# A warmed-up start, a reordered first group and gating stage, and the norms' logarithm taken from PSUM, in a two-block layer on one core

## The chip, the cores and the metric

The kernel runs on one core of one Trainium2 chip. The metric is device time of the whole program in microseconds (us). Before the change it is 2627.98 us, the median of 3 runs (2627.77 to 2628.41).

## What is computed

512 tokens of width 2048 pass through two blocks, all in float32. Cut to what matters:

```
h = rmsnorm(x, norm_mix_g)                       # first block
u = h @ w_in                                     # 12288 columns: c_g b_g xa za q fl iv og ga gb
ya = b_g * dwconv3(c_g * xa) * silu(za)
o  = hgrn2_chunked(silu(q), (1-lb)*sigmoid(-fl), iv, log_f(fl))      # 8 heads of 128
yb = rmsnorm_per_head(o) * hg_norm_g * silu(og)
m  = sigmoid(ga) * (ya @ w_a_out) + sigmoid(gb) * (yb @ w_b_out)
x  = x + m @ w_o
gate = sigmoid(rmsnorm(x, ple_norm_g) @ w_ple_gate)                  # the gating stage
x  = x + gate * (p @ w_ple_proj)
x  = rmsnorm(x, final_norm_g)
mod = silu(c) @ w_ada + b_ada                                        # second block
h = rms_norm(x, g) * (1 + scale) + shift
proj = h @ w_in2                                 # q k v z of 8 attention and 4 retention heads
y = [dilated_attention * silu(z_a), retention (rms-normed per head) * silu(z_r)]
out = rms_norm(x + gate2 * (y @ w_out2), final_gain)
```

rmsnorm(x) is x times the reciprocal square root of (mean of x squared, plus 1e-6), times a gain.

## The kernel before, in words

**Layout.** Everything is kept transposed: the 2048 features lie in 16 tiles ("rows" k) of 128 partitions by 512 tokens. A norm therefore sums over partitions, which TensorE does with a matrix of ones.

**Dense groups.** Each matrix product is cut into groups of 512 output columns, that is four PSUM banks i = 0 to 3 of 128 columns each. A group walks over its input rows k (16 of them as a rule). To keep float32 accuracy with the fast fp32r format, weights and operand are each split into a high and a low part, and each (k, i) takes three matmuls: j = 0 operand-high times weight-high, j = 1 operand-low times weight-high, j = 2 operand-high times weight-low. A group of 16 rows is thus 192 matmuls. `pe_dense` (L299 to 334) writes them; every one has line L329.

**Units.** Weights come in units n of two rows (128 partitions by 1024 elements, 512 KB). SyncE loads a unit into one of four RAW slots, ScalarE casts it into WH (L354; the very first unit in two halves, L347 and L349), VectorE subtracts to get WL (L375, L369). There are three WH/WL slots, so the cast of unit m waits until TensorE has used unit m-3. `hi_upto`, `lo_upto` and `load_upto` (L201 to 211) say how far each engine is to be with its units at step k of group unit n.

**Operand feeds.** The operand of a group is split in the same way: XH on ScalarE, XL on VectorE. For the first group ("fl", half 0) the raw x is fed before its norm is known (L454, L475); ScalarE also squares x (L459) and VectorE adds the squares up (L483), and the factor R0 is put on the result afterwards. From group ("q", 0) on the normed h is fed (L490, L500, L504). A group that is written with `fed=True` takes its rows k = 0 and 1 singly, since they have only just been fed.

**Order.** There is no scheduler at run time. Each engine's program is a Python generator that writes its instructions in a fixed order, and all waits are on semaphores, so an instruction that waits holds up everything behind it on its engine. Side work is woven in by `Turns.after_step`: after each step k of a dense group one piece of the queue `chores` and one piece of the queue `specials` is written. `start_part` (L513) is the special of the start: seven pieces of operand feed, then on ScalarE and VectorE the small work on the bound lb (`bound_act`, `bound_dve`, L540 to 567), then the first norm, then the feed of h.

**Norms.** `rsqrt_act` and `rsqrt_dve` (L402 to 420) share the reciprocal root: VectorE makes m = mean + eps from PSUM (L412), ScalarE takes Ln of m (L406) and Exp of -0.5 times that (L408), and VectorE makes one Newton step in three operations (L415, L417, L420). The table of Ln and Exp is loaded (L64) after the wait for m. Norms are "r0" (start), "hn" (8 heads), "r_ple" (before the gate), "r_12" and "r_1" (after the gating stage), "rn" (4 retention heads); "r_out" (L1752 to 1779) is written out by hand in two halves at the end.

**The gating stage.** Four groups ("gate", g). Behind each, ScalarE makes four sigmoids (L1630), VectorE multiplies and adds them into x (L1922, L1926). For g = 0 to 2 ScalarE then squares each new row twice (L1650), and GpSimd adds the squares into two sums (L2019); there is one pair of buffers, so each square waits for GpSimd's last addition. Only then does ScalarE's program come to the next group's casts. Behind g = 2 VectorE makes five small weight tiles WG (L1929 to 1935). Behind g = 3 ScalarE squares the last four rows (L1637), TensorE sums everything for "r_12" (L399, L1454, L1457) and "r_1", the norm follows, VectorE makes the gains GG and GF (L1939 to 1943), and the feed of the next group ("qr", 0) begins (L1095, L1080, L1100).

## Time and profile before

| | |
|---|---|
| median of 3 runs | 2627.98 us |
| the profiled execution | 2625.84 us, its span 2624.5 us |
| granted TensorE clock, mean | 0.998 |
| VectorE, ScalarE, GpSimd busy | 48%, 34%, 3% of the span |
| DMA | 309 MB, 118 GB/s on average |
| casts of weight units (ScalarE L354) | 443, 1049 ns each |
| low parts of weight units (VectorE L375) | 443, 1230 ns each |

In the profile, PE is TensorE's matmul, PEld its weight load, DVE VectorE, ACT ScalarE, POOL GpSimd and SP SyncE. A matmul's record is longer than its share of the engine, since matmuls overlap: the distance from one start to the next is what counts. The number in brackets behind a row of the timeline is the engine's idle time before the instruction and what ended it. A float32 matmul (not fp32r) shows as two records.

### The profile page before, as it was taken

The page shows a single profiled execution, that of the slowest core. Times are in us where ns is not written, and L with a number is a line of the kernel's source. Part 1 is how long each engine was busy: PE and PEld are TensorE (multiplying, and loading weights), DVE is VectorE, ACT ScalarE, POOL GpSimd, SP SyncE. Part 2 cuts the span into 40 slices and gives each one's busy share as a digit, 9 for nine tenths or more (in the row PEclk, how much of TensorE's full clock was granted, in tenths as well). Part 3 has the DMA queues.
Part 4 walks back from the last instruction along what each step waited for, and adds up shares of the span by engine and source line. Part 5 has one row for each costly group of instructions (what it writes and reads, how often), then busy time and mean ns, then how long its engine had stood idle before and what let it go on. Part 6 is the DMA issues. An engine that isn't in the chain of part 4 may idle for free.

```text
span 2624.5 us, 29678 instructions
## 1 busy us (share of the span) xinstructions
PE 2593.7 (99%) x12166; PEld 2095.4 (80%) x12166; DVE 1265.5 (48%) x2013; ACT 892.0 (34%) x1236; POOL 73.7 (3%) x64
## 2 busy tenths in 40 slices
PE   8999999999999999999999999999999999999998
PEld 7888888878888888888888888688777777777888
DVE  7556634468334555655443453552243434443425
ACT  5643324333222222222322443332232343433323
POOL 0000000000000000000001111100000000000000
PEclk9999999999999999999999999999999999999999
DMA  5322233222334666666442222234222222222424
GB/s 194 101 76 78 81 97 97 89 73 81 89 96 147 217 216 207 216 213 213 136 161 97 94 99 97 73 125 145 85 72 64 89 72 81 73 73 84 165 97 153
DMA packets 159976, 309.18 MB, mean 118 GB/s; under 512 B 11040, under 2 KB 15392, under 8 KB 158816
## 3 DMA queue, kind: packets, MB, share of 16 engines
q1 hardware_dynamic: 159040, 305.70, 36.1%
q8 instruction: 96, 1.57, 0.2%
q0 software_dynamic: 224, 1.15, 0.1%
q10 hardware_dynamic: 576, 0.43, 0.1%
q14 instruction: 40, 0.33, 0.0%
HBM read 298.84 MB, written 8.39 MB: 117 GB/s over the span
## 4 chain that ended last, share of the span: by engine, by line
PE 94%; DVE 2%; issue 2%; ACT 1%; DMA 0%; POOL 0%; SPq 0%; DVEq 0%; ACTq 0%; POOLq 0%
PE bank L329 87%; PE bank L1276 1%; PE bank L1167 1%; PE bank L1250 1%; PE bank L702 1%; PE bank L754 1%; PE bank L1265 1%; PE bank L1156 1%; PE bank L399 0%; DVE WL L375 0%; ACT WH L354 0%; DVE SC L483 0%; DMA X<-in_xT 0%; DVE Y L1980 0%; PE bank L692 0%
## 5 line engine op out<-in xcount | busy, mean ns | idle before, releaser
L329 PE MATMUL bank<-XH,WH 128*128 128x512 f32 (+1 forms) x2880 | 1145.6, 398 | 12.2 <-DVE XL L475 5.5
L329 PE MATMUL bank<-XH,WL 128*128 128x512 f32 (+1 forms) x2880 | 1111.7, 386 | 5.5 <-DVE WL L375 5.5
L329 PE MATMUL bank<-XL,WH 128*128 128x512 f32 (+1 forms) x2880 | 1109.9, 385 | 0.0
L375 DVE TENSOR_TENSOR WL<-RAW,WH 128x1024 fp32r<-128x1024 f32 x443 | 544.0, 1230 | 958.1 <-ACT WH L354 957.2
L354 ACT CAST WH<-RAW 128x1024 fp32r<-128x1024 f32 x443 | 463.9, 1049 | 1162.2 <-PE bank L329 1162.0
L329 PEld LDWEIGHTS bank<-XH,WH 128*128 128x128 f32 x2880 | 542.4, 188 | 135.1 <-issue 20.7
L329 PEld LDWEIGHTS bank<-XL,WH 128*128 128x128 f32 x2880 | 542.7, 188 | 119.3 <-issue 15.0
L329 PEld LDWEIGHTS bank<-XH,WL 128*128 128x128 f32 x2880 | 542.1, 188 | 116.9 <-DVE WL L375 7.2
L329 PE MATMUL bank<-WH,XH 128*128 128x512 f32 x384 | 155.6, 405 | 0.0
L329 PE MATMUL bank<-WL,XH 128*128 128x512 f32 x384 | 149.8, 390 | 0.0
L329 PE MATMUL bank<-WH,XL 128*128 128x512 f32 x384 | 149.5, 389 | 0.0
L1016 DVE CUSTOM_DVE_ANT_0 AST<-AST,CB 128x512 f32<-128x512 f32 x192 | 125.3, 687 | 10.8 <-DMA AST<-in_w_ada 10.8
L329 PE MATMUL bank<-YH,WH 128*128 128x512 f32 x256 | 101.0, 394 | 0.0
L329 PE MATMUL bank<-YH,WL 128*128 128x512 f32 x256 | 100.4, 392 | 0.0
L329 PE MATMUL bank<-YL,WH 128*128 128x512 f32 x256 | 99.5, 389 | 0.0
L329 PEld LDWEIGHTS bank<-WH,XL 128*128 128x128 f32 x384 | 72.2, 188 | 17.5 <-issue 3.1
L329 PEld LDWEIGHTS bank<-WH,XH 128*128 128x128 f32 x384 | 72.1, 188 | 17.4 <-issue 3.1
L329 PEld LDWEIGHTS bank<-WL,XH 128*128 128x128 f32 x384 | 72.1, 188 | 15.3
L1354 DVE CUSTOM_DVE_ANT_0 PP<-PP,CM 128x512 f32<-128x512 f32 x32 | 22.2, 692 | 79.9 <-ACT PP L1288 79.9
L1305 ACT COPY PT<-bank 128x512 f32<-128x512 f32 x32 | 18.7, 585 | 116.1 <-PE bank L1265 116.1
L329 PEld LDWEIGHTS bank<-YH,WL 128*128 128x128 f32 x256 | 48.1, 188 | 11.3
L329 PEld LDWEIGHTS bank<-YL,WH 128*128 128x128 f32 x256 | 48.1, 188 | 10.7
(252 smaller groups left out, 1634.5 us busy)
## 6 DMA issues: line engine op xcount, KB each, us to landing
RAW<-in_w_in SPq DMA_DIRECT2D x303, 512.0 KB, 3.6
AST<-in_w_ada SPq DMA_DIRECT2D x192, 256.0 KB, 4.1
RAW<-in_w_out SPq DMA_DIRECT2D x40, 512.0 KB, 3.5
RAW<-in_w_o SPq DMA_DIRECT2D x32, 512.0 KB, 3.5
RAW<-in_w_gate SPq DMA_DIRECT2D x32, 512.0 KB, 3.5
RAW<-in_w_a SPq DMA_DIRECT2D x16, 512.0 KB, 4.2
RAW<-in_w_b SPq DMA_DIRECT2D x16, 512.0 KB, 4.2
XT<-in_xT SPq DMA_DIRECT2D x4, 1024.0 KB, 7.4
```

The lines of the kernel that those rows point to most:

```text
L329: ins = nc.tensor.matmul(bank[b][:, cols], l, r[:, cols], start=first, stop=final)
L354: nc.scalar.copy(WH[:, m % NSPL], RAW[:, m % NRAW]).then_inc(hi.sem, hi.step(m))
L375: nc.vector.tensor_tensor(WL[:, m % NSPL], RAW[:, m % NRAW], WH[:, m % NSPL].bitcast(F32), ALU.subtract).then_inc(lo.sem, lo.step(m))
L702: ins = nc.tensor.matmul(b[y:y + 64, 32 * n:32 * n + 32].rearrange("p (n x) -> p n x", x=h), t, late(t, lev), start=True, stop=True, tile_ ...
L754: ins = nc.tensor.matmul(b[:, 128 * c:512], VN[:, c, 128 * i:128 * i + 128], AT[:, 640 * c:512 * c + 512], start=c == 0, stop=c == 3)
L1016: nc.vector.tensor_tensor_reduce(AST[:, n % 3], AST[:, n % 3], CB[:, q % 2], 1.0, 0.0, ALU.mult, ALU.add, PART[:, n:n + 1]).then_inc(dve.s ...
L1156: nc.tensor.matmul(b[:, :], YY[:, 9 + 2 * r, 128 * c:128 * c + 128], YY[:, 8 + 2 * r], start=True, stop=True).then_inc(side.sem, side.step ...
L1167: ins = nc.tensor.matmul(b[:, :], V2[:, c, 256 * r + 128 * u:256 * r + 128 * u + 128], PT[:, c], start=c == 0, stop=c == 3)
L1250: nc.tensor.matmul(b[:, :], YY[:, h, 128 * i:128 * i + 128], K[:, j], start=True, stop=True).then_inc(side.sem, side.step(("as", h, i)))
L1265: ins = nc.tensor.transpose(b[:, 128 * c:128 * c + 128], PP[:, i % 2, 128 * c:128 * c + 128], IDN[:, :])
L1276: ins = nc.tensor.matmul(b[:, :], Vt[:, c, 128 * j:128 * j + 128], PT[:, c], start=c == 0, stop=c == 3)
L1354: nc.vector.tensor_tensor_reduce(P, P, CM[:, 2, 384 - 128 * i:896 - 128 * i], 1.0, 0.0, ALU.mult, ALU.add, st[:, 2:3]).then_inc(dve.sem, d ...
```

## The change

It does these things:

- It gives the first three units an order of their own (`hi_upto`, `lo_upto`): one unit is cast and subtracted per step k while n < 2.
- Row k = 0 of every `fed` group is written with j outermost: four matmuls of j = 0, then four of j = 1, then four of j = 2. The wait for the operand's low part moves from j = 0 to j = 1.
- TensorE begins with 11 matmuls of 128x128 ones by 128 columns of ones, into a bank that nothing else uses then.
- The start's feed is spread over ten pieces instead of seven, with one row less of lead (`ahead` 1 instead of 2), the squares of x have four buffers instead of two and are written one row later, and the first norm is written before the work on the bound instead of after it.
- Norms: ScalarE's Ln reads the sum in PSUM, with scale and with eps as a bias from a small tile EPSV; VectorE's m is written after a wait for that Ln. The table load is written before the wait.
- The gating stage: the squares of g = 0 to 2 become a chore woven into the next group; the WG tiles become a chore of the second group; GG and GF are made before the first gate group.

```diff
 def hi_upto(n, k):
+    if n < 2:
+        return k + 1
     return min(n + AHEAD if n or k else 0, len(UNITS) - 1) + 1
 def lo_upto(n, k):
-    return min(hi_upto(n, k), n + AHEAD + k % 2 if n else 3)
+    return hi_upto(n, k) if n < 2 else min(hi_upto(n, k), n + AHEAD + k % 2)
...
-            if fed and k < 2:
-                work = [(k, i) for i in range(4)]
+            if fed and k == 0:
+                work = [(0, i, (j,)) for j in range(3) for i in range(4)]
+            elif fed and k == 1:
+                work = [(1, i, (0, 1, 2)) for i in range(4)]
...
-                for j, (l, r) in enumerate(pairs):
+                for j in parts:
+                    l, r = pairs[j]
                     if j == 0:
...
-                        T.wait_ge(xlo, (yield xlo, (ready, kk)))
...
+                    if j == 1:
+                        T.wait_ge(xlo, (yield xlo, (ready, kk)))
...
-    def rsqrt_act(key, m, y):
-        A.wait_ge(dve, (yield dve, (key, "m")))
+    def rsqrt_act(key, scale, y, eps=0):
         A.use(LNEXP)
-        nc.scalar.activation(y, m, ACT.Ln).then_inc(act.sem, act.step((key, "ln")))
+        A.wait_ge(side, (yield side, (key, "sum")))
+        A.wait_ge(dve, (yield dve, "eps"))
+        nc.scalar.activation(y, bank[banks[key]][:, :], ACT.Ln, bias=EPSV[:, eps:eps + 1], scale=scale
+                             ).then_inc(act.sem, act.step((key, "ln")))
...
     def rsqrt_dve(key, scale, m, y, t, eps=EPS):
-        V.wait_ge(side, (yield side, (key, "sum")))
+        V.wait_ge(act, (yield act, (key, "ln")))
...
+    SQ_AT = (0, 1, 3, 4)
...
-            for j in range(k - 1 if k else 16, 16 if k == 15 else k):
-                if j > 2:
-                    A.wait_ge(dve, (yield dve, ("acc0", j - 2)))
-                nc.scalar.activation(SC[:, j % 2 if j else 2], X0[:, j], ACT.Square
+            for j in range(max(k - 2, 0) if k < 11 else k - 1, 16 if k == 15 else k if k > 9 else k - 1):
+                if j > 4:
+                    A.wait_ge(dve, (yield dve, ("acc0", j - 4)))
+                nc.scalar.activation(SC[:, SQ_AT[j % 4] if j else 2], X0[:, j], ACT.Square
...
     def start_part(eng, bound, norm):
-        for n in range(7):
+        for n in range(10):
             if eng in raw_feed:
-                yield from raw_feed[eng].upto(min(16, 2 * n + 4))
-            yield
-        if bound:
-            yield from bound
-        yield
+                yield from raw_feed[eng].upto(2 * n + 2 if n < 4 else 4 + (4 * n + 1) // 3)
             yield
         if eng == "pe":
             yield
         yield from norm
         yield
+        if bound:
+            yield from bound
...
     def pe():
+        T.wait_ge(dve, (yield dve, "ones"))
+        for n in range(11):
+            nc.tensor.matmul(bank[7][:, 0:128], ONES[:, :], ONES[:, :], start=True, stop=True)
...
-        yield from act_dense(("fl", 0), raw_feed["act"])
+        yield from act_dense(("fl", 0), raw_feed["act"], 1)
...
-            for i in range(4):
-                j = 4 * g + i
-                A.wait_ge(dve, (yield dve, ("x2", j)))
-                if g == 3:
+            if g < 3:
+                turns.chores.append(squares_act(g))
+                continue
+            yield from turns.finish(turns.chores)
...
+    def squares_act(g):
+        for j in range(4 * g, 4 * g + 4):
+            A.wait_ge(dve, (yield dve, ("x2", j)))
+            for u in range(2):
+                scale = vcol("fin_g", j) if u else 1.0
...
+                    if j > 1:
+                        A.wait_ge(pool, (yield pool, ("acc2u", u, j - 1)))
...
+                nc.scalar.activation(dst, X1[:, j], ACT.Square, scale=scale
+                                     ).then_inc(act.sem, act.step(("sq2u", u, j)))
+            yield
+            yield
...
     def out_norm_act(h):
-        A.wait_ge(dve, (yield dve, ("r_out", h, "m")))
-        nc.scalar.activation(N2[:, 1, HALF[h]], N2[:, 0, HALF[h]], ACT.Ln
+        A.wait_ge(side, (yield side, ("r_out", h, "sum")))
+        nc.scalar.activation(N2[:, 1, HALF[h]], bank[banks["r_out", h]][:, HALF[h]], ACT.Ln, bias=EPSV[:, 0:1],
...
     def out_norm_dve(h):
-        V.wait_ge(side, (yield side, ("r_out", h, "sum")))
+        V.wait_ge(act, (yield act, ("r_out", h, "ln")))
...
+        nc.vector.memset(EPSV[:, 0:1], EPS).then_inc(dve.sem, dve.step())
+        nc.vector.memset(EPSV[:, 1:2], EPS * EPS).then_inc(dve.sem, dve.step("eps"))
...
+        V.wait_ge(dve, (yield dve, "mod"))
+        nc.vector.tensor_scalar(GG, MOD[:, 16:32], 1.0, None, ALU.add).then_inc(dve.sem, dve.step("gg0"))
...
+        nc.vector.tensor_tensor(GF, GG, vall("fin_g"), ALU.mult).then_inc(dve.sem, dve.step("gf"))
         for g in range(4):
...
-            if g == 2:
-                nc.vector.tensor_scalar(WG[:, 4], ONES[:, :], EPS, None, ALU.mult
...
+            if g == 0:
+                turns.chores.append(last_weights_dve())
+        yield from turns.finish(turns.chores)
```

`last_weights_dve` waits four steps and then makes the same nine small operations, two or three a step. Squares of the last four rows stay where they were, directly behind the sigmoids of g = 3.

## Rows read from the trace of the kernel before

**Rows 1.** Page, part 1: busy time, share of the span, instructions of each engine.

```profile
PE 2593.7 (99%) x12166; PEld 2095.4 (80%) x12166; DVE 1265.5 (48%) x2013; ACT 892.0 (34%) x1236; POOL 73.7 (3%) x64
```

**Rows 2.** Waits of PE: total us, times, longest us.

```profile
PE bank L329 <- DVE WL L375: 5.5, 4, 2.3
PE bank L329 <- DVE XL L1100: 4.7, 2, 4.3
...
PE bank L329 <- ACT WH L354: 0.5, 2, 0.3
```

**Rows 3.** Timeline, the start and two small float32 matmuls: start us, us, instruction.

```profile
0.84 0.17 DVE L1818 MEMSET ONES<- 128x128 f32 x1 [0.84 <-PEq L2158]
...
4.42 0.60 ACT L347 CAST WH<-RAW 128x512 fp32r<-128x512 f32 x1
...
5.53 0.77 PE L329 MATMUL bank<-XH,WH 128*128 128x512 f32 x1 [5.53 <-DVE XL L475]
...
9.50 0.40 PE L329 MATMUL bank<-XH,WH 128*128 128x512 f32 x1
...
174.33 0.38 PE L719 MATMUL bank<-XX 128*128 128x128 f32 x2
174.55 0.39 PE L720 MATMUL bank<-XX 128*128 128x128 f32 x2
```

**Rows 4.** Windows: span, busy us (x records) of each engine, PEclk, DMA share, GB/s.

```profile
5.50:9.50 4.00, 3.97 (x10) 3.14 (x10) 1.95 (x4) 2.61 (x5) 0.00 (x0) 1.00 1.04 392
...
1699.00:1702.40 3.40, 3.40 (x8) 2.75 (x9) 3.40 (x5) 1.45 (x2) 0.00 (x0) 0.51 0.00 0
...
1505.80:1549.80 44.00, 44.00 (x195) 36.42 (x195) 26.29 (x34) 19.16 (x27) 0.00 (x0) 1.00 0.31 108
```

**Rows 5.** Timeline, first group: the stop near its end, and the first row of h.

```profile
35.17 0.39 PE L329 MATMUL bank<-XL,WH 128*128 128x512 f32 x1
...
37.87 0.51 PE L329 MATMUL bank<-XH,WL 128*128 128x512 f32 x1 [2.31 <-DVE WL L375]
...
45.86 1.29 DVE L500 TENSOR_TENSOR X<-X,R 128x512 f32<-128x512 f32 x2
```

**Rows 6.** Timeline, the third gate group's start, and GpSimd in the stage's last.

```profile
1603.63 2.92 ACT L354 CAST WH<-RAW 128x1024 fp32r<-128x1024 f32 x3
...
1606.60 0.50 PE L329 MATMUL bank<-XH,WL 128*128 128x512 f32 x1 [1.15 <-DVE WL L375]
...
1640.31 10.65 POOL L2019 TENSOR_TENSOR AC<-AC,SQ 128x512 f32<-128x512 f32 x8 [34.85 <-ACT SQ L1650]
```

**Rows 7.** Timeline, the norm "r_12" behind the gating stage.

```profile
1685.78 2.41 ACT L1637 ACTIVATE SQ<-X 128x512 f32<-128x512 f32 x4
...
1690.43 0.69 DVE L412 TENSOR_SCALAR NN<-bank 128x512 f32<-128x512 f32 x1 [2.91 <-PE bank L1457]
1691.15 1.28 ACT L64 ACT_TABLE_LOAD   x1 [2.96 <-DVE NN L412]
1692.44 0.63 ACT L406 ACTIVATE NN<-NN 128x512 f32<-128x512 f32 x1
...
1693.77 0.69 DVE L415 TENSOR_TENSOR NN<-NN 128x512 f32<-128x512 f32 x1 [2.64 <-ACT NN L408]
...
1695.83 0.17 DVE L1939 TENSOR_SCALAR SM<-MOD 128x16 f32<-128x16 f32 x1
...
1696.45 1.41 DVE L1095 SCALAR_TENSOR_TENSOR GT<-X,SM,NN 128x512 f32<-128x512 f32 x2
1697.24 1.38 ACT L1080 ACTIVATE XH<-GT,MOD 128x512 fp32r<-128x512 f32 x2 [2.57 <-DVE GT L1095]
...
1699.00 0.70 PE L329 MATMUL bank<-XH,WH 128*128 128x512 f32 x1 [4.31 <-DVE XL L1100]
```

**Rows 8.** Timeline, the last norm, second half.

```profile
2613.51 0.42 DVE L1769 TENSOR_SCALAR N<-bank 128x256 f32<-128x256 f32 x1 [1.68 <-PE bank L1504]
2613.97 0.42 ACT L1758 ACTIVATE N<-N 128x256 f32<-128x256 f32 x1 [1.69 <-DVE N L1769]
```

More of the change, by code:

```diff
@@ L304, in pe_dense @@
             s = n % NSPL
-            if fed and k < 2:
-                work = [(k, i) for i in range(4)]
-            else:
-                work = [(k - k % 2 + j, i + k % 2 * 2) for i in range(2) for j in range(2)]
-            for q, i in work:
+            if fed and k == 0:
+                work = [(0, i, (j,)) for j in range(3) for i in range(4)]
+            elif fed and k == 1:
+                work = [(1, i, (0, 1, 2)) for i in range(4)]
+            else:
+                work = [(k - k % 2 + j, i + k % 2 * 2, (0, 1, 2)) for i in range(2) for j in range(2)]
+            for q, i, parts in work:
                 kk = kmap[q] if kmap else q
@@ L330, in pe_dense @@
                     done = [(name, i)] * (j == 2 and q == nk - 1)
-                    done += [("unit", n)] * (j == 2 and k % 2 == 1 and (q, i) == work[-1])
+                    done += [("unit", n)] * (j == 2 and k % 2 == 1 and (q, i) == work[-1][:2])
                     if done:
@@ L820, in hgrn_act @@
         yield
-        yield from rsqrt_act(("hn", hh), XX[:, 0], XX[:, 1])
+        yield from rsqrt_act(("hn", hh), 1.0 / 128, XX[:, 1])
         yield
@@ L1204, in retention_act @@
         yield
-        yield from rsqrt_act(("rn", r), TN[:, 2], TN[:, 3])
+        yield from rsqrt_act(("rn", r), 1.0 / 256, TN[:, 3])
         left.discard(r)
@@ L1631, in act_program @@
                                      ).then_inc(ev_a.sem, ev_a.step((("gate", g), i)))
[L1632 to L1652 removed]
+            if g < 3:
+                turns.chores.append(squares_act(g))
+                continue
+            yield from turns.finish(turns.chores)
+            A.wait_ge(dense, (yield dense, (("proj", 3), 3)))
+            for i in range(4):
+                A.wait_ge(dve, (yield dve, ("x2", 12 + i)))
+                nc.scalar.activation(SQ2[:, 2 + i], X1[:, 12 + i], ACT.Square
+                                     ).then_inc(act.sem, act.step(("sq2", 12 + i)))
+        yield from rsqrt_act("r_12", 1.0 / D, R12, 1)
         turns.specials.append(first_norm_act())
@@ L1752, in act_program @@
                 yield from to_end(out_norm_act(1))
+    def squares_act(g):
[3 more added lines that the diff above has]
+                scale = vcol("fin_g", j) if u else 1.0
+                if j == 0:
+                    A.wait_ge(side, (yield side, ("r_ple", "sum")))
+                    dst = AC[:, u]
+                else:
+                    A.wait_ge(dense, (yield dense, (("proj", 3), 3)))
+                    if j > 1:
+                        A.wait_ge(pool, (yield pool, ("acc2u", u, j - 1)))
+                    dst = SQ2[:, u]
+                nc.scalar.activation(dst, X1[:, j], ACT.Square, scale=scale
+                                     ).then_inc(act.sem, act.step(("sq2u", u, j)))
+            yield
+            yield
     def out_norm_act(h):
@@ L1808, in first_norm_act @@
         yield from idle(4)
-        yield from rsqrt_act("r_1", NN[:, 0], R1)
+        yield from rsqrt_act("r_1", 1.0 / D, R1)
     def first_norm_dve():
@@ L1814, in first_norm_dve, with last_weights_dve @@
         yield from rsqrt_dve("r_1", 1.0 / D, NN[:, 0], R1, NN[:, 2])
+    def last_weights_dve():
+        yield from idle(4)
+        nc.vector.tensor_scalar(WG[:, 4], ONES[:, :], EPS, None, ALU.mult
+                                ).then_inc(dve.sem, dve.step())
+        for i in range(4):
+            nc.vector.tensor_scalar(WG[:, i], ONES[:, :], vcol("fin_g", 12 + i), vcol("fin_g", 12 + i),
+                                    ALU.mult, ALU.mult).then_inc(dve.sem, dve.step(("wg", i)))
+            V.wait_ge(dve, (yield dve, ("wg", i)))
+            nc.vector.tensor_scalar(WG[:, i], WG[:, i], EPS, None, ALU.add
+                                    ).then_inc(dve.sem, dve.step(*(["wg"] if i == 3 else [])))
+            yield
     def dve_program():
```

45 lines of the change are left out of this document (10 added, 35 removed).

## The prediction, made before the changed kernel was run

> **What bounds the kernel now.** I read the page first: TensorE is busy 99% of the span [rows 1]. So the kernel can gain only where TensorE stands still or runs slowly, and where its end is followed by a tail. The waits of PE come next. They are few: low parts of weights (L375) stop it four times, ScalarE's casts (L354) twice, the low part of an operand behind the gating stage (L1100) twice [rows 2]; the first matmul starts only at 5.53 [rows 3]. The timeline then puts each in its place. Of the four stops by L375, one of 2.31 us is in the first group [rows 5] and three are in the gating stage, with both stops by L354 [rows 6]; of L1100's 4.7 us, 4.31 is the norm "r_12" [rows 7].
>
> Two things are not in a list of waits. In full flow a matmul takes 0.226 us (44.00 us by 195) [rows 4]. From 5.53 to 9.50 [rows 3] there are nine intervals, 0.44 each; the window's PEclk says 1.00 there, but the ten records in 4 us say half speed [rows 4]. Behind the stop of 4.31 us, eight matmuls fill 3.40 us, and there PEclk says 0.51 [rows 4], that is 1.2 of 2.4 GHz. The stop of 2.31 us was followed by nothing of the kind: the row behind it is 0.51 long, as a first one after a stop is, against 0.39 [rows 5]. So TensorE starts slowly after 5.5 and 4.3 us of standing still, and not after 2.3. A stop costs its idle time and some 0.27 more: from 35.17 to 37.87 is 2.70, less 0.226 is 2.47 against 2.31 idle, and 0.12 for the longer first record [rows 5].
>
> **The start.** The 11 added matmuls need only ONES, ready at 1.01 [rows 3]. A float32 matmul of 128 columns takes 0.22 at full speed (174.33 to 174.55, two records each) [rows 3], so twice that, 0.44, at half: 11 of them end at 1.1 + 4.8 = 5.9 if all are slow. If full speed comes as it did at 9.50, some 4.0 us behind the first matmul, it comes at 5.1, nine are slow and two fast, and they end near 5.4 (estimate). The first real matmul no longer waits for the operand's low part; it needs the high part of the weights, ready at 5.02 [rows 3]. I take 5.4: 0.1 us gained (ends: 0.4 later, 0.5 earlier), and the nine slow intervals gone: 3.97 - 9 x 0.226 = 1.94. At full speed the group asks more of its feeds. It wants row 1 at 5.4 + 2.7 = 8.1 and rows 2 and 3 at 10.8; with units 1 and 2 cast one by one instead of together, unit 1's low part is ready near 9.4, and a gap there would be under 0.5.
>
> The stop at 37.87 goes if unit 5's low part comes in time. Before, VectorE wrote all 16 rows of feed and then unit 5; now only 12 rows stand ahead of it, four fewer at about 1.3 us (a low part and an addition). Taken off the 37.87, that is 32.7, and TensorE asks at 5.4 + 10 x 2.72 + 0.45 = 33.1; the shorter queues of ScalarE (four square buffers) help too. Gain 2.47 + 0.12 = 2.6; low end 1, should unit 5 or 6 still come 1 to 1.5 us late.
>
> The norm's place gives a new wait. VectorE and ScalarE now stand at the norm while unit 7's low part is behind it. From the sum's being visible that takes 0.73 (Ln), 0.66, 3 x 0.72 and 1.2 for the unit, 4.8 in all; TensorE needs it two steps and a part later, 5.4 + 0.45, and 0.2 of hand-over go off: 0.9 to spare. The feed of h began at 45.86 [rows 5] and will begin at about the same time, since the bound's ten small operations, some 0.2 us each as L1939's 0.17 [rows 7], now follow the norm, while group ("q", 0) starts 4.6 us earlier. Its first low parts of weights have 0.7 to 0.8 us left by my count of the queue. I take no stop; 0.5 to 1 of one is the low end. Sum of the start: 0.1 + 1.9 + 2.6 = **4.6** (2.5 to 5.1).
>
> **The gating stage.** At 1603.63 ScalarE casts three units in a row. Units fall due 5.4 us apart (24 matmuls), so the first could have come some 9 us sooner; the squares had held it, each waiting for GpSimd's addition of 1.33 us (10.65 by 8) [rows 6]. With the squares woven in, the cast comes right behind the sigmoids, and the next squares, two every second step (5.4 us), need 2.7 us of GpSimd: no wait left. VectorE's nine WG operations leave the boundary behind g = 2; in the second group they stand before units that are due two units later. All five stops go: 5.5 - 2.3 = 3.2 by L375, 0.5 by L354 [rows 2], 5 x 0.27: **5.0** (4 to 5.1). GG and GF, 0.6 us on VectorE, move ahead of the gate groups, where low parts of the operand are several rows ahead.
>
> **The norm "r_12".** Now: the sum is there at 1690.43, m, then a table load at 1691.15, Ln at 1692.44, Newton at 1693.77, GG at 1695.83, first gained row at 1696.45, its high part at 1697.24, matmul at 1699.00 [rows 7]. After: the squares end at 1688.19 [rows 7], the load (1.28) fits before 1690.43; Ln and Exp take 1.33 as between 1692.44 and 1693.77, plus 0.07 for the bias operand, which no row prices (I take it between nothing and 0.15); Newton starts at 1691.8, and three steps of 0.72 later, without GG and GF, the gained row starts at 1694.0. Its high part starts 0.79 later as now and takes 0.72; with 0.2 of hand-over TensorE starts at 1695.7, as it no longer waits for the low part, which is ready when four matmuls are done. Gain **3.3** (2.3 if it does have to wait for the low part).
>
> ScalarE's page of the Trainium skill, "ScalarE: Activation LUTs", section What ACT_TABLE_LOAD costs, speaks against part of this: a switch costs 1283 ns and some 1380 ns of drain. By it the table would be ready at 1690.85 and the gain 0.4 smaller. The trace agrees on 1.28 but shows no drain: Ln starts 0.01 behind the load [rows 7].
>
> TensorE's sums of "r_1" end at 1694.7, so the stop shrinks from 4.31 to about 1.0, well below the 2.31 that left it fast: the slow stretch goes too, 3.40 - 8 x 0.226 = **1.6**. The second stop by L1100, 0.4 and 0.27, stands behind "r_1", whose chain on VectorE gets shorter by the 1.3 us (Ln and Exp) it waits between m and Newton: **0.6**.
>
> **The tail.** In the last norm Ln starts when m does now, 2613.51 instead of 2613.97 [rows 8]; less 0.1 for the bias: **0.4**, all on the path. The other norms lie beside dense groups in which TensorE never waits: nothing. The j-outermost order asks for the fourth bank of a group 1.4 us earlier; in group "wb", the only one that takes banks of the group just before, its fourth bank was that group's second, complete 12 matmuls (2.7 us) before the start, and a read takes some 0.6: nothing.
>
> **Sum.** 4.6 + 5.0 + 3.3 + 1.6 + 0.6 + 0.4 = 15.5. The profiled execution, 2625.84 with a span of 2624.5, would become 2610.3 and 2609.0. It lies 2.1 under the median of the runs, and I take the difference off that: 2627.98 - 15.5 = **2612.5**.
>
> **Rivals.** (a) The warm-up does not warm: small matmuls leave the clock low, they end at 5.9 and the first nine real ones are slow as before. Gain 15.5 - 1.9 - 0.5 = 13.1: 2614.9. For it: no row shows what 128-column matmuls do to the clock. Against: they fill the engine from 1.1 on. Chance 0.12. "TensorE: Matmul & The Clock Gate", Part 1, in the Trainium skill says that the number of slow matmuls varies from run to run with the phase of the gate. By that this term scatters; a single profile of before cannot show it. (b) The first group becomes VectorE's: with TensorE 4.6 us ahead, unit 5, 7 or 8 stops it as before, 2 to 3 us. For it: VectorE is the engine that stopped it at 37.87, and my slack is under 1 us at three places. Against: it has idle time in which to catch up. 2612.5 + 2.5 = 2615.0. Chance 0.18. (c) A part of what is said does not come: one gating stop stays or "r_12" gains only half. 2614 to 2618. Chance 0.13. (d) Slower: the squares woven in stand ahead of the casts, in all three later gate groups, and wait there for GpSimd. Each of 12 pieces has at most 2.7 us of additions to wait for, and a cast has some 9 us before TensorE needs it. To cost more than the 15.5 gained, 12 pieces would have to bring 1.3 us each past that slack, so each wait would be above 10 us. It decides only if VectorE's x2 rows came a whole unit late, which they do at no boundary now. Some 2633 with a wait of that size. Chance 0.02. (e) The edits do nothing for the time because something else stops TensorE at the same places: within 0.2%. Chance 0.03.
>
> **The numbers.** The likeliest case, as worked out, has 0.52. A run of this kernel can be told from no change at about 0.2%, 5.3 us; all of (a) to (c) are faster than that. So faster 0.95, same 0.03, slower 0.02. The range: above, it takes in (a), (b) and most of (c), 2618.0; below, the upper ends of the terms (0.5 at the start, a bit in the small stops) and some scatter of the median, 2610.0.
>
> **What would show it.** Right: first real matmul near 5.4 at 0.23 intervals; no stop above 0.3 us before 60 us; in the waits of PE no L354 and no L375 in the gating stage; casts directly behind the sigmoids; a table load before the sum and a stop under 1.3 us before ("qr", 0), with PEclk near 1 behind it; Ln straight behind the last sum. Wrong: intervals of 0.43 behind the warm-up (a), a wait for L375 between 8 and 60 us (b), squares ahead of a late cast (d), or new waits of TensorE for banks at the first row of a `fed` group.

## The result, and the profile after

The changed kernel takes **2613.57 us**, the median of 4 runs (2612.94 to 2613.85), beside 2628.19 for the kernel before in the same session (4 runs, 2627.77 to 2630.15). The ratio is 0.9943, with a 95% interval of 0.9925 to 0.996. That is 14.6 us less; forecast were 15.5 less and 2612.5. The two profiled executions differ by less: 2625.84 and 2613.68, that is 12.2, and their spans by 12.7 (2624.54 and 2611.86). The text below works with this 12.7 of span and comes back to the difference between 14.6 and 12.2.

The page of the changed kernel, part 1 (busy time, share of the span, instructions; before: [rows 1]):

```profile
PE 2595.7 (99%) x12188; PEld 2097.1 (80%) x12188; DVE 1260.2 (48%) x2015; ACT 889.0 (34%) x1236; POOL 79.0 (3%) x64
```

TensorE is now busy for 2.0 us longer than before, with a span that is 12.6 shorter. Eleven small matmuls of at most 0.43 us are 4.7 of that; but nine slow intervals at the start and eight behind "r_12" have gone, 3.5 together. Something else has become longer.

The waits of PE in the changed kernel (total us, times, longest; before: [rows 2]):

```profile
PE bank L1273 <- ACT PP L1305: 2.0, 2, 1.0
PE bank L336 <- DVE Y L2006: 1.5, 2, 1.2
PE bank L1415 <- DVE EPSV L1850: 1.1, 1, 1.1
PE bank L336 <- issue: 0.9, 1, 0.9
```

L336 is the dense matmul (L329 before). No wait for weights' low parts (now L382) or casts (L361) is left, and none for the operand's low part. The first two stops, in the attention stage and the last groups, are not touched by the change; the third is the start of the program; 0.9 is what remains of the 4.31 at "r_12".

The timeline of the changed kernel at its start (start us, us, instruction; before: [rows 3]), and VectorE's low part of unit 5 (before: in [rows 5] as the releaser of the stop):

```profile
1.06 5.00 PE L1415 MATMUL bank<-ONES 128*128 128x128 f32 x22 [1.06 <-DVE EPSV L1850]
...
4.64 0.60 ACT L354 CAST WH<-RAW 128x512 fp32r<-128x512 f32 x1
...
5.77 1.22 PE L336 MATMUL bank<-XH,WH 128*128 128x512 f32 x4
6.83 1.09 PE L336 MATMUL bank<-XL,WH 128*128 128x512 f32 x4
7.76 1.10 PE L336 MATMUL bank<-XH,WL 128*128 128x512 f32 x4
...
29.60 1.22 DVE L382 TENSOR_TENSOR WL<-RAW,WH 128x1024 fp32r<-128x1024 f32 x1
```

All 11 warm-up matmuls went at half speed: 4.71 us from 1.06 to 5.77, 0.43 each. The real ones are fast nearly from the first: four in 1.06, then four in 0.93. The weights' high part had been ready at 5.24, so it was the warm-up that the first real matmul waited for.

The timeline of the changed kernel at "r_12" (before: [rows 7]), and a window behind it (span, then busy us and records of each engine, PEclk, DMA share, GB/s; before: [rows 4]):

```profile
1682.94 1.28 ACT L64 ACT_TABLE_LOAD   x1
...
1685.18 0.69 ACT L414 ACTIVATE NN<-bank,EPSV 128x512 f32<-128x512 f32 x1 [0.95 <-PE bank L1468]
...
1686.56 0.69 DVE L424 TENSOR_TENSOR NN<-NN 128x512 f32<-128x512 f32 x1
...
1688.74 1.41 DVE L1103 SCALAR_TENSOR_TENSOR GT<-X,SM,NN 128x512 f32<-128x512 f32 x2
1689.53 1.39 ACT L1088 ACTIVATE XH<-GT,MOD 128x512 fp32r<-128x512 f32 x2 [2.06 <-DVE GT L1103]
1690.28 0.75 DVE L1108 SCALAR_TENSOR_TENSOR XL<-GT,MOD,XH 128x512 fp32r<-128x512 f32 x1
1690.35 1.17 PE L336 MATMUL bank<-XH,WH 128*128 128x512 f32 x4 [0.92 <-issue]
1691.35 1.08 PE L336 MATMUL bank<-XL,WH 128*128 128x512 f32 x4
```

```profile
1690.30:1693.70 3.40, 3.35 (x15) 2.79 (x16) 3.40 (x6) 1.99 (x3) 0.00 (x0) 1.00 0.00 0
```

In the first, the table load stands before the sum, Ln directly behind it, and the operand's low part is begun only 0.07 before the first matmul, which no longer waits for it. Fifteen matmuls in 3.40 us at PEclk 1.00 stand where there were eight at 0.51.

Where the 12.7 come from is seen by laying the starts of the same groups in the two traces beside each other:

| stretch | lead gained, us | predicted |
|---|---|---|
| first matmul (5.77) | -0.24 | +0.1 |
| the rest of the first two groups (to 95.1) | 3.57 | 4.5 |
| to 824 | 0.53 | 0 |
| 824 to 1505.7: eight groups "wa"/"wb" and the projection | **-3.72** | 0 |
| gating stage, "r_12", "r_1" (to 1777.5) | 10.74 | 10.5 |
| attention stage and last groups | 1.36 | 0 |
| tail | 0.44 | 0.4 |

The norm, gating and tail terms fit. A loss of 3.7 us stands where the change edits nothing. One such group, first the kernel before, then the changed one (windows from the group's first matmul to the next group's):

```profile
827.95:849.94 21.99, 21.99 (x97) 18.05 (x96) 12.32 (x24) 5.31 (x6) 0.00 (x0) 1.00 0.71 228
```

```profile
824.09:846.50 22.41, 22.41 (x97) 18.02 (x96) 12.37 (x24) 5.32 (x6) 0.00 (x0) 1.00 0.71 226
```

The same 96 matmuls, the same clock, no idle time in either, and 0.42 us more: 0.2334 instead of 0.2290 for each. What the change did here is hidden in its memory layout. EPSV takes 32 bytes, and the region behind it, W0, moves from byte 127424 to 127456 of each partition. These groups' operands YH and YL lie in W0, as do those of the first group.

### The profile page after: what moved, and what is told of

It reads as the page before. It is cut to its first block, busy times and chain, and to the rows that moved or that the text cites. A ratio compares the mean times of both kernels' runs of the same rounds, so it can differ in the third digit from the quotient of the medians.

```text
span 2611.9 us, 29663 instructions
## 1 busy us (share of the span) xinstructions
PE 2595.7 (99%) x12188; PEld 2097.1 (80%) x12188; DVE 1260.2 (48%) x2015; ACT 889.0 (34%) x1236; POOL 79.0 (3%) x64
## 4 chain that ended last, share of the span: by engine, by line
PE 99%; DVE 1%; ACT 0%; issue 0%
PE bank L336 91%; PE bank L1175 1%; PE bank L1284 1%; PE bank L1258 1%; PE bank L710 1%; PE bank L762 1%; PE bank L406 1%; PE bank L1273 1%; PE bank L1164 1%; PE bank L1415 0%; DVE Y L2006 0%; PE bank L700 0%; PE bank L718 0%; DVE X L1803 0%; PE bank L732 0%; PE bank L1515 0%
## 5 line engine op out<-in xcount | busy, mean ns | idle before, releaser
L336 PE MATMUL bank<-XH,WH 128*128 128x512 f32 (+1 forms) x2880 | 1135.3, 396 | 2.4 <-DVE Y L2006 1.5
L336 PE MATMUL bank<-XH,WL 128*128 128x512 f32 (+1 forms) x2880 | 1102.1, 385 | 0.0
L336 PE MATMUL bank<-XL,WH 128*128 128x512 f32 (+1 forms) x2880 | 1102.0, 385 | 0.0
L382 DVE TENSOR_TENSOR WL<-RAW,WH 128x1024 fp32r<-128x1024 f32 x443 | 543.2, 1227 | 959.3 <-ACT WH L361 958.3
L361 ACT CAST WH<-RAW 128x1024 fp32r<-128x1024 f32 x443 | 463.6, 1047 | 1191.3 <-PE bank L336 1187.3
L336 PEld LDWEIGHTS bank<-XH,WH 128*128 128x128 f32 x2880 | 540.8, 188 | 124.8 <-issue 16.9
L336 PEld LDWEIGHTS bank<-XL,WH 128*128 128x128 f32 x2880 | 541.0, 188 | 118.7 <-issue 15.1
L336 PEld LDWEIGHTS bank<-XH,WL 128*128 128x128 f32 x2880 | 540.7, 188 | 108.8
L336 PE MATMUL bank<-WH,XH 128*128 128x512 f32 x384 | 155.3, 404 | 0.0
L336 PE MATMUL bank<-WL,XH 128*128 128x512 f32 x384 | 149.6, 390 | 0.0
L336 PE MATMUL bank<-WH,XL 128*128 128x512 f32 x384 | 149.4, 389 | 0.0
L336 PE MATMUL bank<-YH,WL 128*128 128x512 f32 x256 | 100.1, 399 | 0.0
L336 PE MATMUL bank<-YL,WH 128*128 128x512 f32 x256 | 99.0, 394 | 0.0
L336 PE MATMUL bank<-YH,WH 128*128 128x512 f32 x256 | 98.5, 393 | 0.0
L336 PEld LDWEIGHTS bank<-WH,XL 128*128 128x128 f32 x384 | 72.1, 188 | 17.6 <-issue 3.1
L336 PEld LDWEIGHTS bank<-WH,XH 128*128 128x128 f32 x384 | 72.1, 188 | 17.3 <-issue 3.1
L336 PEld LDWEIGHTS bank<-WL,XH 128*128 128x128 f32 x384 | 72.1, 188 | 15.1
L336 PEld LDWEIGHTS bank<-YL,WH 128*128 128x128 f32 x256 | 48.1, 188 | 12.4
L336 PEld LDWEIGHTS bank<-YH,WH 128*128 128x128 f32 x256 | 48.1, 188 | 11.4
```

The source lines that it names most:

```text
L336: ins = nc.tensor.matmul(bank[b][:, cols], l, r[:, cols], start=first, stop=final)
L361: nc.scalar.copy(WH[:, m % NSPL], RAW[:, m % NRAW]).then_inc(hi.sem, hi.step(m))
L382: nc.vector.tensor_tensor(WL[:, m % NSPL], RAW[:, m % NRAW], WH[:, m % NSPL].bitcast(F32), ALU.subtract).then_inc(lo.sem, lo.step(m))
```

## The experiments

Each expectation sets a theory against a rival. The first four runs ask about the memory layout.

### The layout

**e1_aligned**, the changed kernel with W0 moved on by another 32 bytes:

```diff
-    W0 = C0 + 3712 + 4 * NVEC
+    W0 = C0 + 3744 + 4 * NVEC
```

> The changed kernel with one number altered: the region W0 begins 64 bytes behind where it began before the change, instead of 32. Theory A (address): the 32-byte shift that made room for EPSV costs every matmul whose moving operand lies behind W0 some 4.4 ns; these are the first group (192), the eight wa and wb groups (768) and the four proj groups (96), 1056 matmuls, 4.6 us. Then a wa or wb group takes 21.99 us again instead of 22.41, the lead over the kernel before no longer falls from 3.86 to 0.54 us between 828 and 1309, and the whole is 4 to 5 us faster than the changed kernel, near 2609. Rival B (order): the groups are slower through the new order of the other engines' work, or through the chip of that run; then a wa group still takes 22.41 and the time stays near 2613.5.

Measured: 2615.23 us (2614.85 to 2616.07), ratio 0.9953 [0.9938, 0.9968]. The group "wa" takes as long as in the changed kernel:

```profile
824.48:846.87 22.39, 22.39 (x98) 18.02 (x96) 12.37 (x24) 5.33 (x6) 0.00 (x0) 1.00 0.72 226
```

Some 2609 was forecast: that the operand only needs a rounder start address is refuted. From 1777 to 2206, where the changed kernel gained 0.94, this one lost 0.64: the layout does act, but not by that rule.

**e2_before_shift32**, the kernel before with W0 moved by 32 bytes and nothing else:

```diff
-    W0 = C0 + 3680 + 4 * NVEC
+    W0 = C0 + 3712 + 4 * NVEC
```

> The kernel before with W0 alone moved by 32 bytes. Theory A (address): wa and wb groups take 22.41 us instead of 21.99, the first group loses 0.8 us, proj 0.4; the whole 4 to 5 us slower than before, near 2632.5, a ratio of 1.0017. Rival B (order): nothing changes, 2628 within 0.5.

Measured: 2630.2 us (10 runs, 2628.42 to 2632.28) beside 2627.82 (13 runs, 2626.31 to 2630.77); ratio 1.0007 [0.9997, 1.0017]. That is 2.4 more, where 4 to 5 were forecast, and the ratio alone can't tell it from nothing; the trace can. Against the kernel before it loses 3.72 from 829 to 1511; it gains 0.53 between 100 and 829, and 1.4 from 1795 on (0.94 of them by 2224). All of these are what the changed kernel shows, within 0.02. So the loss belongs to the 32 bytes, not to the edits. The forecast had left out the two gains.

**m1_addresses** measures it by itself. It leaves out the whole computation: 16 fp32r matmuls in a row of one 128x128 weight by 128x512 from one start address, then two small ones, then the next address.

```diff
+        for off in offs:
...
+            for i in range(16):
+                ins = T.matmul(bank[i % 4][:, :], W[:, :], big[key][:, off // 4:off // 4 + 512], start=True, stop=True)
+            for i in range(2):
+                ins = T.matmul(bank[4][:, 0:64 + 64 * i], W[:, :], big[key][:, 0:64 + 64 * i], start=True, stop=True)
```

> The cost by itself: a kernel that only runs fp32r matmuls of 128x512, sixteen in a row per start address of the moving operand, with nothing else at work; it leaves out the whole computation. Addresses: 57472 (where XH lies in the kernels) plus 0, 64, ... 2048 bytes and some others, and 127424 (W0 before the change) plus 0, 32 (the change), 64 (the run with W0 64 bytes on) and others. The runs so far showed 0.2269 us a matmul with the operand in XH, 0.2290 with W0 as before, 0.2334 with W0 32 or 64 bytes on, so alignment to 64 bytes is not it. Theory A2 (place in memory alone): the same three values, or the same order of them, appear here, by the start address modulo some power of two. Rival C (contention): the address matters only by which bank of the memory other engines are writing at the time; then all addresses give the same value here, 0.22 to 0.227.

Its timeline, for starts 128, 192, 0, 64 and 128 behind a multiple of 256 bytes:

```profile
25.81 3.85 PE L52 MATMUL bank<-Near,Wt 128*128 128x512 f32 x16
29.50 0.33 PE L54 MATMUL bank<-Near,Wt 128*128 128x64 f32 x2
29.67 3.89 PE L52 MATMUL bank<-Near,Wt 128*128 128x512 f32 x16
33.40 0.33 PE L54 MATMUL bank<-Near,Wt 128*128 128x64 f32 x2
33.57 3.94 PE L52 MATMUL bank<-Near,Wt 128*128 128x512 f32 x16
37.35 0.33 PE L54 MATMUL bank<-Near,Wt 128*128 128x64 f32 x2
37.52 3.95 PE L52 MATMUL bank<-Near,Wt 128*128 128x512 f32 x16
41.30 0.33 PE L54 MATMUL bank<-Near,Wt 128*128 128x64 f32 x2
41.47 3.85 PE L52 MATMUL bank<-Near,Wt 128*128 128x512 f32 x16
45.16 0.33 PE L54 MATMUL bank<-Near,Wt 128*128 128x64 f32 x2
```

From a row of 16 to the pair behind it, by 16: 0.2306 at 128, 0.2331 at 192, 0.2363 at 0, 0.2363 at 64, and 0.2306 at 128 again. The pattern repeats every 256 bytes; starts at 32, 160 and 224 take 0.2362 to 0.2374, in this buffer or in a second one at 127424. The first matmul of a row, behind the small pair, is followed only after 0.28 to 0.29, and that is in these averages. From the third to the fifteenth the step is 0.2267 at 128 in this buffer (0.2276 to 0.2284 in the other), 0.2291 at 192, and 0.2325 to 0.2345 at all other starts. These are the steps of the kernels: 0.2267, 0.2290 and 0.2334 (below and above). Nothing else runs here, so work of other engines is out as the cause, and a matmul's time depends on where its moving operand starts: W0 stood at 192 before (second best), at 224 after, at 0 in e1.

**e10_w0_128** puts W0 at 128, the best place:

```diff
-    W0 = C0 + 3712 + 4 * NVEC
+    W0 = C0 + 3872 + 4 * NVEC
```

> The changed kernel with the region W0 moved from byte 127456 to 127616, so that it starts at 128 behind a multiple of 256 (192 in the kernel before, 224 in the changed one). Theory A, the start address of the moving operand modulo 256 sets the distance of two matmuls: the operands YH and YL of the eight groups wa and wb then go at the 0.227 us of XH, 96 matmuls take 21.8 instead of 22.4, and 1056 matmuls gain up to 1056 x 0.0065 = 6.9 us against the changed kernel's 2613.6; the attention stage, whose operands move along, may give back up to 1.6. So 2607 to 2610. Rival B, the matmuls of these groups are slow for another reason (what else runs beside them, the bank they write): the groups stay at 22.4 and the time at 2613 or above.

Measured: **2608.08 us** (2607.78 to 2608.6), ratio 0.9925 [0.9908, 0.9941]. The group that took 21.99 before and 22.41 after:

```profile
823.10:844.86 21.76, 21.76 (x97) 18.02 (x96) 12.28 (x24) 5.31 (x6) 0.00 (x0) 1.00 0.73 231
```

That is 0.2267 for each matmul. Between 823 and 1498 this kernel gains 2.43 on the kernel before, where the changed kernel lost 3.72. Part is given back: it gets neither the 0.53 before 824 nor the 0.94 of the attention stage (there -0.23). One base address moves many operands, and they don't agree on the best one. Theory A holds; this version beats both kernels, 5.5 us under the changed one by the medians (two sessions, whose medians of the kernel before were 0.2 apart) and 5.4 by the spans. Of these, 0.5 is a first matmul at 5.31 instead of 5.77, which the address does not explain.

### The start

**e3_no_warm**, without the warm-up:

```diff
-        T.wait_ge(dve, (yield dve, "ones"))
-        for n in range(11):
-            nc.tensor.matmul(bank[7][:, 0:128], ONES[:, :], ONES[:, :], start=True, stop=True)
```

> The changed kernel without the 11 warm-up matmuls. My theory: the first real matmul starts some 0.4 to 0.6 us earlier (5.2 instead of 5.77) and the first nine or so run at 0.43 us intervals, 1.9 us lost: the span is 1.3 to 1.6 us longer. Rival: the warm-up is worth nothing, because the feeds of the first rows set the pace in the first 12 us anyway; then TensorE reaches row 2 at the same time (within 0.3) with or without it, and the span is the same.

Measured: 2614.43 us (2614.08 to 2614.61), ratio 0.995 [0.9935, 0.9964].

```profile
5.06 2.07 PE L336 MATMUL bank<-XH,WH 128*128 128x512 f32 x4 [5.06 <-ACT WH L354]
6.93 1.91 PE L336 MATMUL bank<-XL,WH 128*128 128x512 f32 x4
8.63 1.15 PE L336 MATMUL bank<-XH,WL 128*128 128x512 f32 x4
```

Eight slow intervals, but a start at 5.06. At 96 us it is 0.92 behind the changed kernel, as it is in the medians (0.86): the warm-up is worth 0.9, less than expected, since it wins some 1.7 of slow intervals and gives 0.7 back by a later first matmul.

**e12_w0_warm9**, e10 with nine instead of eleven:

```diff
-        for n in range(11):
+        for n in range(9):
```

> The kernel of e10_w0_128 with 9 warm-up matmuls instead of 11. In the changed kernel all 11 ran at half speed and ended at 5.8, 0.7 us behind the high part of the first weights. Theory A, the clock rises a fixed time after TensorE began: with 9 the first real matmul starts at 5.1, the first two or three real ones take 0.43, and the whole is up to 0.3 us faster than e10. Rival B: the rise needs what the last two warm-ups add; then the first real matmuls are slow for longer, and the time is the same or up to 0.5 us longer than that of e10.

Measured: 2608.57 us (2608.23 to 2609.41), ratio 0.9926 [0.9912, 0.9941], no better than e10. The warm-ups end early and TensorE waits 0.59 for the cast of the first weights; it starts at 5.35, and e10, whose clock rose within its warm-ups, at 5.31. Two short stops in the third row (0.17 at 11.48 by the operand's low part, and one at 12.52) then cost 0.8. The first real matmul can't start before the first weights' cast ends, between 5.0 and 5.5 in these traces, whatever TensorE does.

Theory A of this run, a rise of the clock a fixed time after TensorE began, is refuted by the traces together, and the two missing warm-ups did not hold it back either (rival B). In all kernels with a warm-up it begins at 1.05 or 1.06. By the distances of starts full speed came at 4.1 here, at 4.8 in e10, at the end of the warm-ups in the changed kernel, and only at 7.1 in e4 below, where the first four real matmuls take this long (1.22 in the changed kernel):

```profile
5.77 1.80 PE L336 MATMUL bank<-XH,WH 128*128 128x512 f32 x4
```

At 95 us e4 is 0.55 behind the changed kernel, with no edit there. So what a warm-up of this length is worth differs between executions, by up to half a microsecond in these traces.

**e7_old_first_order**, the changed kernel with the whole old order of the first group (units 0 to 2, seven pieces of feed, the lead of two rows, the norm behind the bound):

```diff
 def hi_upto(n, k):
-    if n < 2:
-        return k + 1
...
-    return hi_upto(n, k) if n < 2 else min(hi_upto(n, k), n + AHEAD + k % 2)
+    return min(hi_upto(n, k), n + AHEAD + k % 2 if n else 3)
...
-        for n in range(10):
+        for n in range(7):
...
-                yield from raw_feed[eng].upto(2 * n + 2 if n < 4 else 4 + (4 * n + 1) // 3)
+                yield from raw_feed[eng].upto(min(16, 2 * n + 4))
```

> The changed kernel with the first group's order of before (units, feed pieces, bound ahead of the norm, lead of 2; warm-up, four square buffers and the j order stay). My theory: the stop behind unit 5's low part comes back, 2 to 4 us, longer than before's 2.3 if anything, because TensorE now runs the group 2 us earlier. Rival: the warm-up and the four square buffers alone were enough; the stop stays under 0.5 us.

Measured: 2615.67 us in one run; 1.9 behind the changed kernel at 95 us, though its first matmul was 0.4 earlier (5.37).

```profile
12.55 0.50 PE L334 MATMUL bank<-XH,WH 128*128 128x512 f32 x1 [1.33 <-ACT WH L359]
12.89 0.39 PE L334 MATMUL bank<-XL,WH 128*128 128x512 f32 x1
13.81 0.50 PE L334 MATMUL bank<-XH,WL 128*128 128x512 f32 x1 [0.53 <-DVE WL L380]
```

The stop that I expected behind unit 5 came at unit 1 instead. With TensorE fast from the start, the old order gives it the weights of rows 2 and 3 too late; in the kernel before, where TensorE was itself slow for 4 us, nothing stopped it there. The delay then hides what unit 5 would have cost: its low part is begun at 34.31 and ready at 35.52, and TensorE asks for it at 36.31. The changed kernel asks at 34.37, so at its pace the stop would be some 1.2 us (estimate).

**e11_two_square_buffers**, the old buffers and rows for the squares of x:

```diff
-            for j in range(max(k - 2, 0) if k < 11 else k - 1, 16 if k == 15 else k if k > 9 else k - 1):
-                if j > 4:
-                    A.wait_ge(dve, (yield dve, ("acc0", j - 4)))
...
+            for j in range(k - 1 if k else 16, 16 if k == 15 else k):
+                if j > 2:
+                    A.wait_ge(dve, (yield dve, ("acc0", j - 2)))
...
```

> The changed kernel with the old two buffers for the squares of x, each square written in its old row. Theory A, the stop of 2.31 us behind weight unit 5 was ended by the squares holding up ScalarE's and VectorE's queues, not by the order of units 0 to 2: a stop of 1 to 3 us by a low part of weights or by a cast comes back between 25 and 45 us, and the lead over the kernel before at 95 us falls from 3.3 to 0.5 to 2.3. Rival B, the spread of the operand feed over ten pieces is what removed it: no stop above 0.3 us there, the lead at 95 us stays at 3.0 to 3.3.

Measured: 2613.74 us in one run; at 95 us 0.57 behind the changed kernel.

```profile
30.79 1.22 DVE L382 TENSOR_TENSOR WL<-RAW,WH 128x1024 fp32r<-128x1024 f32 x1
```

Unit 5's low part is 1.2 us later than with four buffers and still in time; there is no stop. In both, VectorE has made the low parts of 12 rows of x before it, in the kernel before and in e7 those of all 16. So theory A is refuted, and the order of the feed is what is left. That stays argued: e7 took this order back, but its TensorE came too late to need unit 5 early. Of the 0.57, 0.2 are slower first matmuls and 0.4 a later sum of the first norm (40.00).

**e8_j_inner**, row 0 of the `fed` groups in the old order of j:

```diff
-            if fed and k == 0:
-                work = [(0, i, (j,)) for j in range(3) for i in range(4)]
-            elif fed and k == 1:
-                work = [(1, i, (0, 1, 2)) for i in range(4)]
+            if fed and k < 2:
+                work = [(k, i, (0, 1, 2)) for i in range(4)]
```

> The changed kernel with j innermost again in row 0 of the fed groups; the wait for the low part stays at j = 1. My theory: the stop in front of qr is as long (0.9), but behind its first matmul TensorE waits some 0.7 us for the first low part; at the start it costs nothing, as the low parts are there when the warm-up ends. In all 0.5 to 1.0 us slower. Rival: the low part is ready by then and nothing changes.

Measured: 2614.33 us in one run. In the trace 0.9 are lost within the first 60 us, half of them within the first four matmuls, where the third waits for the weights' low part (I had forecast nothing there), and 0.5 at "qr":

```profile
1690.95 0.47 PE L334 MATMUL bank<-XH,WH 128*128 128x512 f32 x1 [0.91 <-issue]
1691.69 0.50 PE L334 MATMUL bank<-XL,WH 128*128 128x512 f32 x1 [0.27 <-DVE XL L1106]
```

TensorE stops for the low part right behind its first matmul, as forecast; the j-outermost order costs nothing anywhere.

### The gating stage and the norm

**e4_squares_back**, the squares directly behind the sigmoids again:

```diff
-                turns.chores.append(squares_act(g))
+                yield from to_end(squares_act(g))
```

> The changed kernel with the squares of the first three gate groups written directly behind the sigmoids again (WG stays a chore). My theory: the squares are what holds the casts, so the five stops come back but the third boundary's longest, to which the WG work added, is like the second's: stops of 0.2, 0.3, 1.15, 0.3 and 1.2 us with 0.27 each, 4.4 us in all. Rival: without the WG work VectorE catches up and the stops stay under 2 us in all.

Measured: 2618.3 us in one run. Its waits of PE:

```profile
PE bank L336 <- DVE WL L382: 2.5, 3, 1.2
...
PE bank L336 <- ACT WH L361: 0.5, 2, 0.3
```

All five stops are back, three for low parts, two for casts; only the one in the last gate group is shorter than before (1.16 for 1.80). From 1505 to 1782 the lead grows by 6.21 instead of 10.73: the squares' place is worth 4.5. Of the 10.7, "r_12" and "r_1" have 5.6 (below). The last 0.6 is the shorter stop in the last gate group (1.16 for 1.80), where the WG tiles had stood in the way; no run moved them back alone.

**e5_ln_from_m**, Ln from VectorE's m, the table load behind the wait, as before:

```diff
     def rsqrt_act(key, scale, y, eps=0):
...
+        A.wait_ge(dve, (yield dve, (key, "m")))
         A.use(LNEXP)
...
+        nc.scalar.activation(y, m, ACT.Ln).then_inc(act.sem, act.step((key, "ln")))
```

> The changed kernel with the norms as before: Ln from m, the table load behind the wait (GG and GF stay ahead of the gate groups; the last norm keeps its new form). My theory: the stop in front of group qr grows from 0.9 to about 2.9 us (0.7 for m, 1.3 for the table load, less the longer bias operand), which is just about where TensorE may or may not slow down; if it does not, the whole is 2 us slower, if it does, 3.6. The stop behind r_1 may come back, 0.3. Rival: the gain at r_12 came from GG and GF and the relaxed wait for the low part, and the norms' form gives under 1 us.

**e6_load_first**, the same with the table load ahead of the wait:

```diff
     def rsqrt_act(key, scale, y, eps=0):
...
         A.use(LNEXP)
...
+        A.wait_ge(dve, (yield dve, (key, "m")))
+        nc.scalar.activation(y, m, ACT.Ln).then_inc(act.sem, act.step((key, "ln")))
```

> The changed kernel with the logarithm taken from VectorE's m again, as before, but the table load still written ahead of the wait for m. In the run that undid both (e5_ln_from_m) 3.9 us were lost at the norm r_12, of them some 1.6 by eight slow matmuls behind a stop of 2.86 us. Theory A, the table load of 1.28 us is most of it and m 0.7 the rest: here 0.6 to 0.8 us are lost at r_12, the stop is 1.6 us and nothing slow is behind it; in all 2614.5 to 2615. Rival B: m costs more because the hand-overs between the engines count too, 1.2 us or more are lost; or the stop of 1.6 us brings slow matmuls as the one of 1.8 us did in a run before, then 2.2 or more.

Measured, one run each: 2617.34 and 2614.08 us. First e5's timeline and window, then e6's:

```profile
1686.17 1.28 ACT L64 ACT_TABLE_LOAD   x1 [2.98 <-DVE NN L422]
1687.47 0.63 ACT L416 ACTIVATE NN<-NN 128x512 f32<-128x512 f32 x1
...
1692.58 1.95 PE L336 MATMUL bank<-XH,WH 128*128 128x512 f32 x4 [2.86 <-issue]
```

```profile
1692.55:1696.05 3.50, 3.47 (x9) 2.74 (x10) 3.50 (x6) 2.04 (x3) 0.00 (x0) 0.52 0.00 0
```

```profile
1690.92 1.17 PE L336 MATMUL bank<-XH,WH 128*128 128x512 f32 x4 [1.58 <-issue]
```

The stop is 0.92 in the changed kernel, 1.58 with m in the way, 2.86 with the load behind it as well: m costs 0.66 and the load 1.28, each its own duration and no more. Behind 2.86 us eight matmuls go at half speed, another 1.6; that makes 3.5 of the 3.9 that e5 loses here. Behind 1.58 all are fast. The last 0.3, lost in e6 too, is the second stop, behind "r_1" (in e6 at 1713.89). So the norms' new form is 1.94 of the 3.39 by which the stop at "r_12" shrank, and the rival that it gives under 1 us is out. The other 1.45 belong to GG and GF and to the relaxed wait for the low part; no run took back GG and GF, and e8 took back only the order of j.

## Why the prediction was right, and where it was not

**The start, 4.6 forecast, 3.3 measured.** Full speed behind the warm-up and no stop to 60 us came as said; rivals (a) and (b) are out, as are (c) to (e): no forecast stop stayed, and none came. Unit 5's low part was ready at 30.82, not at 32.7, behind the 12 rows that I had counted, and TensorE asked for it at 34.37, not at 33.1. "I take 5.4" for the first matmul was wrong, 5.77: I let the clock rise within the warm-ups, and in this execution it rose at their end. In e10's it rose earlier (11 in 4.25 us), in e4's later (7.1): this term was taken from one trace and scatters. The Trainium skill, "TensorE: Matmul & The Clock Gate", Part 1, says that the number of slow matmuls varies from run to run; the traces agree: 9 slow ones in the kernel before, 10 in e2, all 11 small ones here. The later first matmul is 0.3 of the missing 1.3; another 0.8 is the layout, 192 x 0.0044: between 14 and 34 us the first group's steps are 0.2333 instead of 0.2289.

**The gating stage and "r_12", 10.5 forecast, 10.7 measured**, by the steps given: squares 4.5 (e4), the WG tiles 0.6 (together 5.1; 5.0 forecast); the stop from 4.31 to 0.92 (3.4; 3.3 forecast), the slow stretch 1.6, and the second stop, of "r_1", 0.6. Ln from PSUM with a bias operand takes 0.06 more than from m (0.69 against 0.63); m costs 0.66 (e6), the load 1.28 (e5 less e6). The Trainium skill, "ScalarE: Activation LUTs", What ACT_TABLE_LOAD costs, adds 1380 ns of drain to a table switch; no trace here shows it, and in e5 Ln starts 0.02 behind the load. The tail gave 0.44 for 0.4.

**What no step had.** I costed EPSV at nothing. It was the dearest line of the change: 32 bytes in front of W0 cost 0.8 in the first group and 3.7 in the groups behind 824, and gave back 0.5 before 824 and 1.4 from 1777 on, net 2.7 us; the loss and both gains stand in e2's trace, without any of the other edits. 15.5 less 2.7 is 12.8, against the 12.7 of the two spans.

**That the number still fitted** is partly luck: by the profiled pair the saving was 3.3 us less than forecast, by the medians 0.9 less. The medians differ by 14.6, which is 2.4 more than the profiled pair's 12.2. The profiled execution of the kernel before, 2625.84, is below every timed run of it (2626.31 to 2630.77 in all), while the changed kernel's runs lie within 1 us. I had taken the saving off the median unchanged, as though the stops cost the same in every execution. They may not. In e2's trace the last gating stop by a weights' low part, 1.80 us in the kernel before, reads (timeline, then the window behind it):

```profile
1657.98 0.50 PE L329 MATMUL bank<-XH,WL 128*128 128x512 f32 x1 [1.81 <-DVE WL L375]
...
1659.36 0.63 PE L329 MATMUL bank<-XL,WH 128*128 128x512 f32 x1
1659.78 0.63 PE L329 MATMUL bank<-XH,WL 128*128 128x512 f32 x1
```

```profile
1659.36:1662.85 3.49, 3.49 (x10) 2.77 (x9) 0.83 (x1) 0.00 (x0) 0.00 (x0) 0.55 0.89 298
```

Five matmuls behind the stop the clock fell: nine intervals fill 3.64 us (1659.01 to 1662.65) instead of 2.0, so 1.6 more. In the profiled execution of the kernel before it did not. So "slowly after 5.5 and 4.3 us of standing still, and not after 2.3" was drawn from too few stops. Such stretches in some executions would explain both the scatter of the kernel before and the 2.4 us, since the changed kernel has no gating stop left to bring one. The timed runs speak for it. The record gives the mean granted clock of each execution, and a stretch of 3.4 us at half speed takes 0.0006 off the mean over 2627 us. Of the 21 executions of the kernel before that were timed beside the experiments, the five at 0.998 took 2626.31 to 2626.81 us, the fifteen at 0.997 took 2627.59 to 2629.39, and the one at 0.996 took 2630.77; the profiled one, 2625.84, had 0.998. So the spread goes with the clock. Where the slow stretches lay in those executions is not shown, since no run profiled the same kernel many times.

## What to carry to other kernels

In a kernel that TensorE fills, compare the starts of the same groups in both traces before believing a sum: a new 8-byte tile in front of a large region can move a thousand matmuls to a worse start address. Put moving operands where short runs show them to be fastest, and re-measure, since operands in one region may want different places. What the clock adds to a stop differs between executions, so a single profile doesn't price it: look at the granted clock of the timed runs too.

## What the runs showed of the hardware that I had not expected

- A 128x512 fp32r matmul takes 0.227 us from a start 128 bytes behind a multiple of 256, 0.229 from 192, and 0.2325 to 0.2345 from 0, 32, 64, 160 and 224, with nothing else running (m1). In the kernels the steps are 0.2267, 0.2290 and 0.2334 for 128, 192 and 224 (e10, before, after). Why is open.
- The granted clock fell after stops of 1.81 (e2), 2.86 (e5) and 4.31 us, and not after 1.80 and 2.31 (before), 1.91 (e2) or 1.58 (e6). Work had begun again by then: since 0.1 us in the kernel before and in e5, since 1.1 us at both places in e2.
- With the same warm-up from 1.06 on, full speed came between 4.1 (e12) and 7.1 us (e4). Without it, it came 3.7 us (e3), 4.0 (before) and 4.5 (e2) behind the first matmul.
- GpSimd's additions of squares come to 1.52 us each when woven in by pairs (two in 3.04), against 1.33 in the burst before (8 in 10.65, [rows 6]). In the trace the second of a pair takes 1.28 us, as most of the burst do (1.27 to 1.29); the first, behind a pause, takes 1.8, and in the burst the first two take 1.47 and 1.74. So the longer mean is that of the first ones; no run tried what lengthens them. It costs nothing here:

```profile
1643.66 3.04 POOL L2045 TENSOR_TENSOR AC<-AC,SQ 128x512 f32<-128x512 f32 x2 [1.40 <-ACT SQ L1767]
```
